# Two chained transformer blocks on one core: seams reordered, products of two channel blocks paired in the joinings

## The reference

```python
# first block
z = rmsnorm(x, g_mix) @ w_in                       # MLA, RWKV and gate columns
y_a, y_b = mla_branch(z_mla), rwkv7_branch(z_rwkv) # attention; recurrent scan
gate_a, gate_b = split(sigmoid(z_gate), 2)
x = x + (gate_a * y_a + gate_b * y_b) @ w_out
x = x + square(relu(rmsnorm(x, g_ffn) @ w_ffn_up)) @ w_ffn_down
x = x + sigmoid(rmsnorm(x, g_ple) @ w_ple_gate) * (p @ w_ple_proj)
x = rmsnorm(x, g_final)
# second block
proj = rms_norm(x, g_mix_2) @ w_in_2               # u_a, u_b, gate logits
y_a = (rglru(conv(u_a), forward) + rglru(conv(u_a), backward)) @ p_a_2      # 1280 -> 1024
pooled = windowed means (2, 4, 8, 16) of u_b minus u_b
y_b = (block_diag(pooled, w_pool, b_pool) * pool_scale) @ p_b_2             # 1024 -> 1024
gates = sigmoid(gate_logits + b_gate)
x = x + (gates[:1024] * y_a + gates[1024:] * y_b) @ w_out_2
up = conv(rms_norm(x, g_ffn_2) @ w_up_2)
x = x + (gelu(up[:2816]) * up[2816:]) @ w_down_2
return rms_norm(x, g_final_2)
```

## Time and profile before

| | |
|---|---|
| median of 3 runs | 3628.96 us (3626.51 to 3631.47) |
| the profiled execution | 3635.13 us, its span 3633.8 us |
| mean granted TensorE clock | 0.98 of full |
| TensorE busy | 3482.7 us (96%), 20382 matmuls |
| VectorE, ScalarE, GpSimd busy | 1786.5 us (49%), 1292.5 us (36%), 1056.6 us (29%) |

### The profile page before, as it was taken

One profiled execution on the slowest core, in us unless ns is written; L12 is line 12 of the kernel. 1 busy time (PEld: TensorE's weight loads), 2 busy tenths in 40 slices (PEclk: granted clock), 3 DMA queues, 4 the chain that ended last, 5 costly groups with the idle time before them and its releaser, 6 DMA issues.

```text
span 3633.8 us, 48527 instructions
## 1 busy us (share of the span) xinstructions
PE 3482.7 (96%) x20382; PEld 2828.5 (78%) x20382; DVE 1786.5 (49%) x2383; ACT 1292.5 (36%) x2197; POOL 1056.6 (29%) x592
## 2 busy tenths in 40 slices
PE   6999999999999999999998989999899999999998
PEld 5888888887677788888886677777687788888886
DVE  4655746337754433333334539874544443434435
ACT  4343433345433322222223547761232333223232
POOL 3212122110033233333331126661343232222221
PEclk9999999999999999999999999999999999999999
DMA  4101101110045211111111322223454311111111
GB/s 139 47 23 42 49 21 45 50 33 7 1 161 172 67 47 50 50 47 47 52 53 64 110 78 80 80 85 104 159 183 145 107 52 48 47 47 52 47 47 53
DMA packets 282377, 253.66 MB, mean 70 GB/s; under 512 B 11621, under 2 KB 221985, under 8 KB 282160
## 3 DMA queue, kind: packets, MB, share of 16 engines
q1 hardware_dynamic: 267552, 216.29, 19.5%
q10 hardware_dynamic: 11520, 25.17, 1.8%
q0 software_dynamic: 3088, 9.10, 0.7%
HBM read 213.81 MB, written 36.70 MB: 69 GB/s over the span
## 4 chain that ended last, share of the span: by engine, by line


## 5 line engine op out<-in xcount | busy, mean ns | idle before, releaser
L406 POOL TENSOR_TENSOR weight_lo<-stage,weight_hi 128x1024 fp32r<-128x1024 f32 (+4 forms) x265 | 626.2, 2367 | 1436.8 <-ACT weight_hi L398 1394.1
L369 PE MATMUL psum<-hT_hi,weight_hi 128*128 128x512 f32 x2240 | 888.8, 397 | 10.4 <-DVE hT_lo L555 7.2
L370 PE MATMUL psum<-hT_lo,weight_hi 128*128 128x512 f32 x2240 | 877.1, 392 | 0.0
L371 PE MATMUL psum<-hT_hi,weight_lo 128*128 128x512 f32 x2240 | 876.3, 391 | 0.0
L369 PEld LDWEIGHTS psum<-hT_hi,weight_hi 128*128 128x128 f32 x2240 | 423.9, 189 | 109.5 <-issue 12.0
L370 PEld LDWEIGHTS psum<-hT_lo,weight_hi 128*128 128x128 f32 x2240 | 424.2, 189 | 91.0 <-issue 4.3
L371 PEld LDWEIGHTS psum<-hT_hi,weight_lo 128*128 128x128 f32 x2240 | 423.6, 189 | 89.3
L398 ACT ACTIVATE weight_hi<-stage 128x1024 fp32r<-128x1024 f32 (+4 forms) x329 | 315.8, 975 | 464.8 <-PE psum L371 411.3
L2045 DVE TENSOR_TENSOR x<-x,psum 128x512 f32<-128x512 f32 x432 | 290.1, 686 | 216.4 <-PE psum L371 215.7
L369 PE MATMUL psum<-weight_hi,act_hi 128*128 128x512 f32 x864 | 339.5, 393 | 0.0
L370 PE MATMUL psum<-weight_lo,act_hi 128*128 128x512 f32 x864 | 339.1, 392 | 0.0
(11 more groups left out here) (376 smaller groups left out, 5288.8 us busy)
## 6 DMA issues: line engine op xcount, KB each, us to landing
stage<-in_w_in SPq DMA_DIRECT2D x64, 512.0 KB, 4.0
stage<-in_w_up SPq DMA_DIRECT2D x44, 512.0 KB, 3.9
scratch_gates<-gate ACTq DMA_DIRECT2D x64, 256.0 KB, 2.0
gs<-scratch_gates SPq DMA_DIRECT2D x64, 256.0 KB, 2.7
stage<-in_w_out SPq DMA_DIRECT2D x32, 512.0 KB, 4.7
stage<-in_w_ffn_up SPq DMA_DIRECT2D x32, 512.0 KB, 4.1
stage<-in_w_ffn_down SPq DMA_DIRECT2D x32, 512.0 KB, 3.7
stage<-in_w_down SPq DMA_DIRECT2D x22, 512.0 KB, 3.5
```

The lines of the kernel that those rows point to most:

```text
L369: q.matmul(out, stat[0], mov[0], start=first, stop=False)
L370: q.matmul(out, stat[0], mov[1], start=False, stop=False)
L371: return q.matmul(out, stat[1], mov[0], start=False, stop=final)
L406: g.q.tensor_tensor(lo, K.staged(w), hi.bitcast(F32), ALU.subtract).then_inc(*S.w_lo_pool.up(w))
```

## The change

The step lists of several stages are written anew; what is computed stays.

- Intro: three gate blocks instead of two, two gate halves instead of four in the first block's preparation; squares and norm factors by halves of the rows; `sig_g` is awaited at its own product.
- Compressed part: the first pair's queries come before the turns of the second part; the heads' turns go head by head, and scores wait for their own head.
- Joinings: in part 0 two channel blocks' first products come before their second ones; tiles are given back after each `gate_sum`; the second part's gates are fetched beside the product with w_out, and half of the norm's factors are reckoned after channel block 4 of the second part.
- First FFN: four blocks of up-projection ahead instead of three. Second FFN: the last two down groups are summed in one bank (`pe_down_pair`), and the last rows go in other groups (`LAST_ROWS`).
- Gated embedding: p and its weights are loaded and turned by halves; the gate products go weight tile by weight tile over four rows of tokens with four banks open, except in the last quarter; each weight tile is given back alone; turns take banks 4 to 7 (ring "upper").
- Pooling: window sums and means are separate steps, the sums of a group's first block coming before the pooled products; the last group's gates, branch fetches and six branch rows come before the last pooled products; the last two pooled blocks are read from SBUF (`direct`) and their stores follow.

```diff
-    K.pe.wait_ge(K.S.act_op, "sig_g")
...
+            K.pe.wait_ge(K.S.act_op, "sig_g")
...
+def direct(m, part, bi, k):
+
+    return (m, part, bi) == (2, 0, 1) and k >= NP - 2
...
+def branch_rows(K, q, m, part, bi, k):
+
+    if direct(m, part, bi, k):
+        q.wait_ge(K.S.dve_evac, ("pool", k, part))
+        return K.yb2[k % 2][:, part * SPAN:(part + 1) * SPAN]
...
+def pe_down_pair(K, g, t, n, w, part):
...
+        mm = three(pe.q, b, [x[:, k0 + k, tc] for x in K.act[2]], (hi[:, k, :], lo[:, k, :]), (part, k) == (0, 0), (part, k) == (1, GRP - 1))
+    if part:
+        mm.then_inc(*S.mm.up(key))
...
+    b = K.open(key, (t % (NT // 2),)) if i == 0 else K.bank(key)
+    K.need_row(3, t)
+    K.need_weight(w)
+    hi, lo = K.weight(w)
+    for k in range(2):
...
-INTRO_GATES = 2
-PREP_GATES = (4, 4, 4, 4)
+INTRO_GATES = 3
+PREP_GATES = (2, 4, 4, 4)
 RWKV_RING = 4
 GATES_AHEAD = 4
+LAST_ROWS = {3: (0, 1, 2), 5: (3, 4), 6: (5,), 7: (6, 7)}
 POOL_GATES = (0, 0, 1, 1)
-FFN_AHEAD = {1: 3, 2: 1}
+FFN_AHEAD = {1: 4, 2: 1}
...
+    def squares(half):
+        for t in range(half * NT // 2, (half + 1) * NT // 2):
+            for n in range(2):
+                o.do("square_in", t, n)
+    squares(0)
+    advance(norm, 3)
+    o.slot(0)
+    advance(norm, 2)
+    o.do("param")
+    o.slot(1)
+    squares(1)
+    advance(norm, 1)
+    for s in range(2, INTRO_GATES + 1):
...
+    pair = order_pair(o, 0, "all")
     for part, n in ((0, NQ), (1, NKV)):
         for t0 in range(0, NT, 4):
             for c in range(n):
                 o.do("cturn", part, t0, c)
+        if part == 0:
+            advance(pair, NT)
...
+    wanted = [(part, j, bi) for part in range(2) for j in range(ND) for bi in range(2)]
+    at = {}
+
+    def fetch(upto=None):
+        while wanted and len(at) < GATE_SLOTS and (upto is None or wanted[0][0] <= upto):
+            gate = wanted.pop(0)
+            at[gate] = next(slot)
+            o.do("gate_load", m, *gate, at[gate])
     for part in range(2):
         last = part == 1
-        wanted = [(j, bi) for j in range(ND) for bi in range(2)]
-        at = {}
-
-        def fetch():
-            while wanted and len(at) < GATE_SLOTS:
-                j, bi = wanted.pop(0)
-                at[j, bi] = next(slot)
-                o.do("gate_load", m, part, j, bi, at[j, bi])
-        fetch()
+
+        def project(j, bi):
+            w, n, loaded = branches[bi]
+            cuts = branch_tiles(n)
+            w0 = o.take(*[weight_block(w, j * P, P, a, b) for a, b in cuts])
+            o.do("project", m, part, j, bi, tuple(range(w0, w0 + len(cuts))))
+            return len(cuts)
+        fetch(part)
+        used = 0
         for j in range(ND):
-            used = ()
-            for bi, (w, n, loaded) in enumerate(branches):
-                cuts = branch_tiles(n)
-                w0 = o.take(*[weight_block(w, j * P, P, a, b) for a, b in cuts])
-                ws = tuple(range(w0, w0 + len(cuts)))
-                used += ws
-                o.do("project", m, part, j, bi, ws, used if bi else ())
-            o.do("gate_sum", m, part, j, at.pop((j, 0)), at.pop((j, 1)))
-            fetch()
-            o.released(len(used))
+            both = part == 0
+            if not both or j % 2 == 0:
+                used = project(j, 0)
+                if both:
+                    used += project(j + 1, 0)
+            used += project(j, 1)
+            o.do("gate_sum", m, part, j, at.pop((part, j, 0)), at.pop((part, j, 1)))
+            fetch(part)
+            o.released(used)
+            used = 0
+            if last and j == ND // 2:
+                o.do("rstd", nid, range(NT // 2))
...
+        elif m == 2:
+            o.do("yb_stored")
...
+                    if (n, w) == (0, 1):
+                        fetch()
...
+        elif f == 2 and i == blocks // GRP - 2:
+            continue
+        elif f == 2 and i == blocks // GRP - 1:
+            last_group()
+            w0 = o.take(*[tile for g in (i - 1, i) for n in range(2) for tile in rows512(down, n, GRP * g, GRP * (g + 1))])
+            for t in range(NT // 2):
+                for n in range(2):
+                    o.do("down_pair", i, t, n, w0 + n, 0)
+            for t in range(NT):
+                for n in range(2):
+                    if t >= NT // 2:
+                        o.do("down_pair", i, t, n, w0 + n, 0)
+                    o.do("down_pair", i, t, n, w0 + 2 + n, 1)
+                    o.do("down_rows", f, i, t, n)
+                block_done(t)
+            o.released(4)
...
+    for half, n in ((0, 0), (0, 1), (1, 0)):
+        w0 = tiles(n)
+        ts = range(half * rows, (half + 1) * rows)
+        for w in range(4):
             for t in ts:
-                o.do("ple_gate", t, n, w0)
-                if t == ts[-1]:
-                    o.released(4)
-                if first:
-                    o.do("p_turn")
-                    first = False
-                o.do("ple_proj", t, n)
-                o.do("ple_mix", t, n)
-                if mix_norm is None:
-                    advance(ple_norm, 0 if (t, n) == (1, 0) else 1)
-                elif 2 <= n * (NT // 2) + t - NT // 2 < 2 + NORM_STEPS:
-                    advance(mix_norm, 1)
-                if n and t % (NT // 2) == 2:
-                    order_rows(o, "x2", (t - 2, t - 1))
-        order_rows(o, "x2", (ts[-1] - 1, ts[-1]))
-        if half == 0:
+                o.do("ple_gate", t, n, w0 + w, w)
+                if w == 3:
+                    end_row(t, n)
+            o.released()
+            if half == 0:
+                advance(ple_norm, 1)
+            elif w in (1, 3):
+                advance(mix_norm, 1)
+        if (half, n) == (0, 0):
+            o.do("p_turn", 1)
+        if (half, n) == (0, 1):
+            order_rows(o, "x2", ts)
             o.do("gain", 4)
...
+    w0 = tiles(1)
+    for t in range(rows, NT):
+        for w in range(4):
+            o.do("ple_gate", t, 1, w0 + w, w)
+        end_row(t, 1)
+        if t % 2:
+            order_rows(o, "x2", (t - 1, t))
...
         if g == 0:
-            o.do("window_load", 0)
-            o.do("window", 0)
+            o.do("counts_load", 0)
+            o.do("wpool_load", 0)
+            o.do("window_sums", 0)
+            o.do("window_mean", 0)
             window_front(1)
-            o.do("window", 1)
+            o.do("window_sums", 1)
+            o.do("window_mean", 1)
+        if last:
+            o.do("branch_fetch", 2, 0, 0, 0, NL)
+            o.do("branch_fetch", 2, 0, 1, 0, NP - 2)
         gates.fill(2 * POOL_GATES[g])
-        if g + 1 == len(WINDOWS):
-            o.do("branch_fetch", 2, 0, 0)
-        for c in (2 * g + 2, 2 * g + 3):
-            if c < NP:
-                window_front(c)
+        if last:
+            gates.close()
+            o.handover()
+            for k in range(6):
+                o.do("branch_load", 2, 0, 0, k)
+        else:
+            window_front(2 * g + 2)
+            o.do("counts_load", g + 1)
+            window_front(2 * g + 3)
+            o.do("window_sums", 2 * g + 2)
         for blk in (2 * g, 2 * g + 1):
             for h in range(NHALF):
                 o.do("pool_out", blk, h)
-        if g + 1 < len(WINDOWS):
-            o.do("window_load", g + 1)
-        for c in (2 * g + 2, 2 * g + 3):
-            if c < NP:
-                o.do("window", c)
-    for k in range(NL):
+            if not last:
+                o.do("pool_store", blk)
+        if not last:
+            o.do("wpool_load", g + 1)
+            o.do("window_mean", 2 * g + 2)
+            o.do("window_sums", 2 * g + 3)
+            o.do("window_mean", 2 * g + 3)
+    for k in range(6, NL):
         o.do("branch_load", 2, 0, 0, k)
-    o.do("yb_stored")
-    gates.close()
-    o.handover()
+    for k in range(NP):
+        o.do("branch_load", 2, 0, 1, k)
+    for blk in range(NP - 2, NP):
+        o.do("pool_store", blk)
...
+        if t in LAST_ROWS:
+            order_rows(o, "out", LAST_ROWS[t])
```

More of the change, by code:

```diff
@@ L3176, in block @@
             yield
[L3177 removed]
+    blocks = [block(c) for c in range(GATES_AHEAD)]
+    for n, b in enumerate(blocks):
+        next(b)
+        advance(mix_norm, (2, 1, 2, 0)[n])
+    finish(mix_norm)
+    for b in blocks:
+        finish(b)
     gates.done = 2 * GATES_AHEAD
```

263 lines of the change are left out of this document (149 added, 114 removed).

## The result

The changed kernel takes **3602.32 us** (median of 4 runs, 3595.60 to 3604.04) against 3629.94 us of the kernel before beside it (4 runs, 3626.51 to 3631.47): a ratio of 0.992 with a 95% interval of 0.9908 to 0.9933, 27.6 us or 0.8% faster. In a later session it measured 3600.39 us, ratio 0.9912 (0.9897 to 0.9927). The prediction was 3590 us, the range 3558 to 3612.

A forecast was written before the change was run, and what follows sets the result against it. TensorE, busy 96%, was taken to bound the kernel: only its 151 us idle, low-clock matmuls and the tail could shrink. Terms summed to 39 us, from 3635.1 to 3596, less the 6.2 us median offset: 3590 us, range 3558 to 3612.

The forecast's parts named there:

- Rival 4: Whole kernel: waits only move to the next in line, TensorE's idle time stays 151 us; 3629 us, 4%.
- The loss: Second joining, first part: four TensorE waits of 6.0 us for the sixth tile, each with a slow-clock stretch; -34 us.
- Rival 1: Second joining: the four stalls don't come, sixth tile split in time or product starts on high parts; 3556 us, 15%.
- Rival 3: Second joining, first part: the clock doesn't come back between the stalls; slower, 3666 us, 4%.
- Windows and the second joining's start: Window sums moved, branch rows fetched and split earlier, last pooled blocks read in place: dc and br_lo waits shrink; +16 us.
- Second part: Second joining: gates fetched during the products before it, so the 5.8 us wait goes with 2.0 of clock; +7.8 us.
- End: After the last matmul: last two down groups summed in the bank, rows finished in smaller groups; +6.5 us.
- Start: Start and first blocks: the 6.5 us wait goes whole, of the other 5.8 a part only moves; +9 us.
- Compressed queries: Compressed queries to attention: cz wait of 3.1 us stays, kT wait and its like are covered; +4 us.
- First joining and up block ahead: First joining's smaller waits, +6 us; one more up-projection block before the first FFN takes most of remaining 3.9, +4.5.
- Gated embedding with hand-over: Tile-wise products and early p loads remove waits, +13.2 and +7.8; hand-over -2; with 0.3 at its start, +19.3 us.
- Rival 2: Gated embedding: seam gains don't come, each tile-wise product needs a row VectorE delivers late; 3609 us, 17%.

The follow-up runs named there:

- experiment 1: Changed kernel with pairs (two first products ahead of the second ones) in the first joining only, none in the second: 3571.19 us, ratio 0.9831 to the kernel before.
- experiment 2: Changed kernel, pairs kept, but in the second joining the first product's two tiles given back right behind it: 3570.80 us, ratio 0.9828 to the kernel before.
- Experiment 3: Kernel before the change with pairs in the second joining's first part and nothing else: 3648.86 us, ratio 1.0048, 16.7 us slower.
- experiment 4: Changed kernel, pairs kept, but VectorE makes the low part of the sixth tile: 3590.94 us, ratio 0.9888 to the kernel before.
- experiment 9: Kernel of experiment 2 with two gate blocks in the intro and four halves in the first preparation, as before the change: 3565.66 us, ratio 0.9814.
- experiment 10: Kernel of experiment 2 with three up-projection blocks ahead in the first FFN instead of four: 3573.32 us, ratio 0.9839.
- experiment 8: Kernel of experiment 2 with the gated embedding's first three quarters row by row again, four tiles given back at once: 3588.64 us, ratio 0.9885.
- experiment 5: Kernel of experiment 2 with four gate halves in the first preparation again, three gate blocks in the intro kept: 3566.60 us, ratio 0.9823.
- experiment 6: Kernel of experiment 2 with two hand-over weight tiles given back early and two gate halves ahead instead of one: 3567.54 us, again 3568.14 us.

## Why the prediction was right, and where it was off

The prediction named the four waits of the second joining, their place, their number and their chain; the forecast's sum was 39 us against 34.0 in the spans. The signs that it gave are there too: the clock at 0.50 behind each wait, the xn wait left at the hand-over, 8.9 us of tail, 5.0 us of idle time in the embedding's first 60 us. Rival 4 (nothing changes) fell with TensorE's idle time, 132.9 instead of 151 us.

- **The loss**, -34: right. Four waits of 5.9 us (6.0 predicted), each followed by 4.6 us at clock 0.50 that cost 2.2 (2.5 predicted), 24.5 us of products and a wait apart. That is 32.5, shown by experiments 1 and 2 from above, 3 from below and 4 on the chain. Rival 1 (no stall) is refuted by the first three. Of the clock the row behind the wait speaks clearly: 1.00 again from 2559.8 on. Rival 3 is refuted with it. The rule of the Trainium skill weighed there (TensorE: Matmul & The Clock Gate, "A second HAM failure mode: psum-queue depth-cycling") ties the swing between the levels to short idles. The trace agrees in the swing, here behind idles of 5.9 us, and shorter ones can do it too, though not each time: a wait of 2.1 us at the joining's start was followed by a stretch at 0.50 in the changed kernel's second profile (2529.6 to 2532.4), and by none in the first, where 2516.0 to 2549.3 us, with waits of 2.2 and 2.1, stayed at 1.00. The four stalls lost one slow stretch each, nothing beyond: behind the first, 22.4 us of products at 1.00 follow.
- **Windows and the second joining's start**, +16: right. 9.6 us lie ahead of its first product (155.5 to 145.8 in the table), and the first part is 25.9 us longer instead of 32.5, so 6.6 lie in it: 16.2. The terms were mixed otherwise: the dc wait went whole (6.4, not 5.1), of the 9.3 us on branch rows 5.0 went, and the rest, some 5 us, is clock. The rule against it (DMA: Bandwidth & Descriptors, "Issuing engines are not separate DMA queues") would have given 13.3; no run here separates the fetches' share.
- **Second part**, +7.8: 8.3, but the cause is in part another, and the number in part luck. Experiment 3 has pairs and stalls in the first part and the gates' loads of before, and its second part is already 4.3 us shorter, the wait on weight_lo 2.1 instead of 5.8. The nine profiles with all of the change but no stalls have waits of 1.6 to 3.2 us there and take 99.8 to 103.1 us, 3.1 to 6.4 less than before; those with stalls (the changed kernel twice, experiment 4) have at most 0.8 us of wait and take 97.9 to 98.9. So the step "gates are fetched during the products before it" does not take the whole wait; the stalls of the first part take the rest.
- **End**, +6.5: 6.7.
- **Start**, +9: 5.9. The step that was mis-sized is "a part only moves". The v wait of 5.4 us in the first block, whose cause (VectorE's chain with 10.9 us less beside it) was named, was put at less than it is. What the text did not see is that the wait on sig_g needed no further gate block at all (experiment 9).
- **Compressed queries**, +4: 4.4 in one profile, 1.8 in the other, and not as described. The cz wait of 3.1, which was to stay, is gone; the kT wait, which was to be covered, grew from 2.0 to 4.3, and one of 3.3 on cT is new. From the scan's last state products to attention's first turn TensorE is idle 8.8 us before and 8.6 in both profiles after: the waits moved. What fell is its busy time, 117.6 us at clock 0.94 before, 113.5 at 0.99 and 116.0 at 0.97 after. Why the clock is higher there stays open.
- **First joining and up block ahead**, +6 and +4.5: together 8.8 (0.2, 5.3 and 3.3), 15.0 in the second profile. "One more up-projection block takes most of the remaining 3.9" is wrong: it takes 1.5 us of waits (experiment 10).
- **Gated embedding with hand-over**, +19.3: 17.1 less 3.1, so 14. Two terms failed. In the first 60 us 5 us of idle time stay, not 2: the wait on the first xn (2.0) was not counted, and that on a p turn's bank is 2.8. The hand-over was put at -2; its waits grew from 11.9 to 14.7 us. Rival 2 (no gain at all here) is refuted by the place itself, 17.1 us shorter, and experiment 8 gives the gain to the tile order.
- **Profile to median**: the remaining 7 of the 12 us between 3590 and 3602. The text took the offset of 6.2 us between the profiled execution and the median over to the changed kernel. It was the chance of one execution: after, the profiled one lies 1.2 us below its median. More than half of the error is this, no mechanism. And the 5 us of the sum are what is left of larger misses of both signs.

## What to carry to other kernels

A group of products may be reordered only as far as the ring's slots reach: count the tiles that the new order needs before the first one is given back, and look at what stands ahead of the next tile's preparation in each engine's order. Here giving two tiles back one product earlier was worth 31.5 us, more than the 27.6 that the whole change had gained. Work that is moved to cover one chain is taken from another (gate halves, experiments 5 and 9), so try the ordering of the wait first and the cover afterwards. The counts of experiment 9 and the hand-over of experiment 6 were not run together; whether they add up stays open.

## Not expected of the hardware

A VectorE instruction with two operands in SBUF can take much longer beside GpSimd: xn of 128x1024 took 3.43 us at the hand-over beside two low parts on GpSimd, and 1.28 us a little later, when GpSimd was idle.

```profile
2043.69 3.43 DVE L531 SCALAR_TENSOR_TENSOR xn<-x,squares,gain 128x1024 f32<-128x1024 f32 x1
2043.69 5.64 POOL L414 TENSOR_TENSOR weight_lo<-stage,weight_hi 128x1024 fp32r<-128x1024 f32 x2 [51.69 <-ACT weight_hi L406]
2052.24 1.28 DVE L531 SCALAR_TENSOR_TENSOR xn<-x,squares,gain 128x1024 f32<-128x1024 f32 x1
```

The Trainium skill (GPSIMD Engine Reference, "1. Specifications") names contention with VectorE instructions that have two SBUF inputs, and the trace agrees; the size, 2.1 us on top of 1.28, is the trace's. TensorE's wait of 7.9 us there ends with this xn, so these 2.1 us seem to be part of it; no run took the low parts away from it.
